# Down weights of the experts issued from ScalarE's DMA queue, gate and up weights from SyncE's

## The reference

```python
def hier_moe(h, ...):
    # top-1 group of 4, then top-2 of the 8 experts in it: gates (tokens x 32)
    for e in range(32):
        hid = silu(t @ w_gate[e]) * (t @ w_up[e])     # (512, 1024) @ (1024, 512), twice
        y = y + gates[:, e:e + 1] * (hid @ w_down[e]) # (512, 512) @ (512, 1024)
```

## Time and profile before

| what | value |
|---|---|
| three runs | 1262.97, 1267.99, 1271.01 us |
| profiled execution: own time / span | 1260.54 / 1258.7 us |
| mean granted TensorE clock | 0.946 |
| busy share of PE, DVE, ACT, POOL | 86, 34, 26, 23 % |
| read from HBM, written | 265.45 MB, 14.63 MB |
| transfers issued by SP (q1) | 114168 packets, 254.15 MB |
| transfers issued by ACT (q10) | 5248 packets, 10.49 MB |
| transfers issued by POOL (q0) | 4992 packets, 13.37 MB |

### The profile page before, as it was taken

How to read it: one execution, slowest core, us unless ns; L and a number is a source line. 1 busy time by engine, 2 the same in 40 slices (tenths; PEclk the granted TensorE clock), 3 DMA queues, 4 the chain that set the end, 5 groups by cost and what they waited for, 6 DMA issues and landing times.

```text
span 1258.7 us, 13952 instructions
## 1 busy us (share of the span) xinstructions
PE 1082.9 (86%) x5506; PEld 695.9 (55%) x5506; DVE 431.1 (34%) x783; ACT 327.9 (26%) x571; POOL 293.1 (23%) x195
## 2 busy tenths in 40 slices
PE   3999999999999999889999559987878878778881
PEld 2778899777789888768867413322222222222220
DVE  3222594488870232359982710000000000000003
ACT  5343642333332544452231301111011011011000
POOL 4332243432224433374440210000000000000002
PEclk8999999999999999999989769999898989889996
DMA  6222223312224522243354749999999999999965
GB/s 155 67 68 67 68 68 101 84 51 67 67 56 146 166 68 68 67 151 100 100 234 200 218 164 402 409 412 419 414 411 418 419 413 415 404 405 412 424 269 207
DMA packets 124455, 278.63 MB, mean 221 GB/s; under 512 B 11561, under 2 KB 97593, under 8 KB 108025
## 3 DMA queue, kind: packets, MB, share of 16 engines
q1 hardware_dynamic: 114168, 254.15, 54.8%
q0 software_dynamic: 4992, 13.37, 3.1%
q10 hardware_dynamic: 5248, 10.49, 2.2%
HBM read 265.45 MB, written 14.63 MB: 223 GB/s over the span
## 4 chain that ended last, share of the span: by engine, by line
PE 60%; DMA 27%; DVE 5%; issue 2%; ACT 2%; POOL 2%; SPq 1%; POOLq 0%; ACTq 0%; DVEq 0%
DMA arena<-w_exp_up_in 25%; PE bank L451 15%; PE bank L472 13%; PE bank L783 10%; PE bank L689 6%; PE bank L746 3%; PE bank L796 2%; DVE work L1239 2%; PE bank L519 1%; PE bank L630 1%; PE bank L587 1%; PE bank L647 1%; POOL piece_r L1614 1%; PE bank L576 1%; DVE piece_r L1348 1%
## 5 line engine op out<-in xcount | busy, mean ns | idle before, releaser
L783 PE MATMUL bank<-arena,work 128*64 128x512 f32 x1024 | 253.7, 653 | 62.5 <-DMA arena<-w_exp_up_in 61.6
L1588 POOL TENSOR_TENSOR piece_r<-arena,piece_r 128x1024 fp32r<-128x1024 f32 x84 | 202.0, 2413 | 384.6 <-ACT piece_r L864 384.6
L451 PE MATMUL bank<-piece_r 128*128 128x512 f32 x960 | 238.0, 399 | 0.0
L783 PEld LDWEIGHTS bank<-arena,work 128*64 128x64 f32 x1024 | 78.8, 150 | 235.3 <-issue 229.2
L451 PEld LDWEIGHTS bank<-piece_r 128*128 128x128 f32 x960 | 175.5, 188 | 41.8 <-issue 7.4
L1502 DVE TENSOR_TENSOR work<-work,bank 128x256 f32<-128x256 f32 x32 | 13.5, 422 | 455.6 <-ACT work L1089 455.6
L472 PEld LDWEIGHTS bank<-piece_r 128*128 128x128 f32 x1344 | 162.1, 192 | 7.4 <-issue 7.4
L472 PE MATMUL bank<-piece_r 128*128 128x256 f32 x1344 | 165.4, 284 | 0.0
L796 PE MATMUL bank<-arena,work 128*64 128x512 f32 x512 | 116.9, 598 | 15.2 <-ACT work L1091 14.7
L864 ACT ACTIVATE piece_r<-arena 128x1024 fp32r<-128x1024 f32 x84 | 88.6, 1057 | 145.1 <-DMA arena<-w_in_in 81.9
L1646 POOL DMA_INDIRECT arena<-h_rows,idx_all x32 | 29.6, 926 | 405.5 <-PE bank L775 402.7
(11 more groups left out here) (230 smaller groups left out, 940.3 us busy)
## 6 DMA issues: line engine op xcount, KB each, us to landing
arena<-w_exp_gate_in SPq DMA_DIRECT2D x32, 2048.0 KB, 31.5
arena<-w_exp_up_in SPq DMA_DIRECT2D x32, 2048.0 KB, 37.9
arena<-w_exp_down_in SPq DMA_DIRECT2D x32, 2048.0 KB, 38.9
arena<-w_in_in SPq DMA_DIRECT2D x68, 512.0 KB, 3.9
y_rows<-work ACTq DMA_DIRECT2D x64, 96.0 KB, 7.6
arena<-w_branch_gla_in SPq DMA_DIRECT2D x8, 512.0 KB, 3.9
arena<-w_branch_dsa_in SPq DMA_DIRECT2D x8, 512.0 KB, 5.1
arena<-w_out_in SPq DMA_DIRECT2D x2, 2048.0 KB, 8.6
```

Source lines behind the costliest of these rows:

```text
L451: last = mm(bank[n % 2][:, :], w[:, k, :], h[:, k, :], start=(i == 0 and k == 0), stop=(i == 2 and k == K - 1))
L783: last = mm(bank[0][hf * WIDE:(hf + 1) * WIDE, :], hTe[sl][:, k, :], wgu[sl][2][:, :, k, hf * HALF:(hf + 1) * HALF], start=(k == 0), stop= ...
L1588: Q.tensor_tensor(quarter(w_lo, q), quarter(w_raw, q), quarter(w_hi, q).bitcast(F32), ALU.subtract).then_inc(s["wlo_ready"], 1)
```

## The change

SP's loop keeps the gate and up loads and loses the wait for `y_ready` and the down load. ACT issues the down load of expert e+3 right behind its wait for `y_ready` of expert e, which is ahead of its wait for `y_stored`, its copy of the product and its two stores. The down loads of experts 0, 1 and 2 stay with SP. ACT's loop is shortened by one round, and its last five experts stand in straight code, the last three of them without a load.

```diff
@@ SP
                 for sl in range(3):
                     sp.wait_ge(s["gu_ready"], e + (sl - 2))
                     load_up(e + sl, sl)
-                    sp.wait_ge(s["y_ready"], e + (sl - 2))
-                    load_down(e + sl, sl)
             for sl in range(2):
                 sp.wait_ge(s["gu_ready"], E3 + sl - 2)
                 load_up(E3 + sl, sl)
-                sp.wait_ge(s["y_ready"], E3 + sl - 2)
-                load_down(E3 + sl, sl)
@@ ACT
-            def run_expert(e, sl, rounds):
+            def run_expert(e, sl, rounds, load_next=True):
...
                 act.wait_ge(s["y_ready"], e + 1)
+                if load_next:
+                    act.dma_start(wdn[sl].rearrange("p (h c) d -> p h c d", h=2),
+                                  wdd[bass.ds(e + 3, 1)].rearrange("e p h c d -> p (e h) c d"))\
+                        .then_inc(wdn_loaded[sl], 16)
                 act.wait_ge(y_stored[sl], rounds * 32 + 32)
                 A(y_sb[sl], bank[1][:, :], ACT.Copy).then_inc(s["act_s"], 1)
                 act.wait_ge(s["act_s"], e + (T + 1))
                 store_y(e * SLOTS, sl, y_stored[sl])
 
-            with act.Fori(0, E3 // 3) as r:
+            with act.Fori(0, E3 // 3 - 1) as r:
                 for sl in range(3):
                     run_expert(r * 3 + sl, sl, r)
-            for sl in range(2):
-                run_expert(E3 + sl, sl, E3 // 3)
+            for e in range(E3 - 3, NE):
+                run_expert(e, e % 3, e // 3, load_next=(e + 3 < NE))
```

## The result

| | us |
|---|---|
| before, median of 18 runs | 1263.35 (1259.52 to 1271.01) |
| changed, median of 18 runs | 1270.24 (1267.82 to 1279.35) |
| ratio, 95% interval | 1.0065 (1.0048 to 1.0081) |
| profiled execution, own time / span | 1268.80 / 1267.0 |

The change costs 0.65% by the ratio, 8.2 us of 1263.35 (6.1 to 10.2); the two medians as they stand are 6.9 us apart. The forecast was +8.9 us, and a span of 1267.6 us. The forecast median of 1277 is 6.8 us too high: 4.6 of them come from the first three runs of before, whose median of 1268 it was added to, and the rest from the 8.9.

A forecast was written before the change was run, and what follows sets the result against it. It took the expert stage to be bound by weight bytes at 411 GB/s, plus PE's work left afterwards. All terms were 0 except the late down loads at the end: 1268.0 + 8.9 = 1277 us median, range 1264 to 1287.

The forecast's parts named there:

- Losing SP's wait gains nothing: SP's loop: dropping the 121.7 us of y_ready waits at L396 issues no gate or up load earlier; worth 0.
- ACT's 29 issues are covered: ACT's expert loop: 29 issues at 0.38 us, 11 us, fit in 6.3 us free per expert; cost 0.
- The bytes end at the same time: Expert stage: the same 201 MB move at 411 GB/s, so weight transfers still end at 1222.5 us.
- The queues take turns, packet for packet, and ACT's queue falls behind: DMA queues: 256 turns of SP's queue pass only 256 of ACT's 352 packets, so down loads fall 96 behind each expert.
- PE pays at the end: Last experts: late down weights leave PE computing alone after the transfers; +8.9 us, bounds -5.8 and +16.2.
- The worked case: PE gets expert 28's down weights at t; transfers end t + 25.5, last down product starts t + 40.2, 1237.2 us.
- first rival: Last experts: down loads get more than needed, up loads come last; +3 to +8 us, 1274 us; chance 0.18.
- The middle costs nothing: Middle of the expert stage: while any queue has work, the bytes lose no time, so PE's waits there cost nothing.
- Down loads ahead: ACT's queue gets more than its need, so up loads come last; +3 to +8 us, 1274 us; chance 0.18.
- Nothing changes: Expert stage: arrival order stays close to need, sum 0, 1268 us; chance 0.12.
- Stores stuck: ACT's queue: stores wait behind down loads and stall ACT, from landings of about 52 us; 1286 us; chance 0.12.
- Faster bytes: Weight transfers: two queues reach 422 GB/s, saving 12.2 us; 1256 us at best, some 1265; chance 0.08.

The follow-up runs named there:

- act_issue_only: Kernel before, plus straight code for ACT's last five experts and a 4 KB dummy DMA issue where the down load would go; ratio 1.0005 to before.
- tail_on_sp: Changed kernel, but SP again issues the down loads of experts 28 to 31, in order of need; ratio 1.0031 to before, stage 479.8 us.
- stores_on_sp: Changed kernel, but SP issues each expert's two stores behind the gate and up loads; ratio 1.0035 to before, stage 484.5 us.
- small_after: Changed kernel, with each gate and up load split in two, 512 pieces of 8 KB per expert; ratio 1.0086 to before, stage 488.5 us.
- store_first: Changed kernel, but ACT issues the down load behind the product's copy and two stores; ratio 1.0057 to before, stage 486.6 us.
- small_before: Kernel before, with each gate and up load split in two, all loads on SP's queue; ratio 0.9999 to before, stage 478.3 us.
- tail_on_act: Kernel before, with only the down loads of experts 28 to 31 moved to ACT; ratio 1.0032 to before, stage 483.9 us.

## Why the prediction was right

Point by point, by its own steps:

- *Losing SP's wait gains nothing.* Right: SP's waits at L392 grew from 263.0 to 421.9 us, more than it had waited at L392 and L396 together (384.7), and a gate load still goes out right behind the product that it waits for (product over at 1191.85, issue at 1191.88).
- *ACT's 29 issues are covered.* Right, by act_issue_only. In the changed kernel they took 0.40 to 0.44 us each, and no long one of 2.7 us occurred.
- *The bytes end at the same time.* Right, 411 GB/s both times, end at 1221.5 against 1222.5 us.
- *The queues take turns, packet for packet, and ACT's queue falls behind.* Right, shown by changing the numbers twice and by the equal counts, 473 against 469. The Trainium skill's page "DMA: Bandwidth & Descriptors", section on queues, rings and completion order, states round robin at packet granularity, with some 9 to 17 descriptors to a packet. Both flips agree with the turns; how many rows make one turn no run here shows, only that it is equally many on both queues. By the rule in its section "Issuing engines are not separate DMA queues", that issuing from several engines only saves sequencer time, the change would have been worth 0: the engines and their throughput are shared as it says, but the time differs by 8 us, since the order of landing is not kept.
- *PE pays at the end.* Right in kind, and in size by the luck of two errors that nearly cancel. The worked case: down product of 28 at t, that of 31 at t + 40.2, transfers over at t + 25.5. Measured with t = 1195.34: t + 41.1 and t + 26.2. Expert 29's down product came 14.56 us behind that of 28, so the late load cost 2.1 us above the pace of 12.44, not 2.9. (The profile's 2.60 us of idle time hold the 0.47 that pass before a down product anyway.) What was left out is the clock: after that wait the product took 5.35 us instead of 3.65 (+1.7), at a granted clock of 0.50 from 1212 to 1214 us, a term the prediction used only in its first rival. 2.1 + 1.7 + 3 x 12.44 are the 41.1. The last down product starts 15.0 us behind the end of the transfers instead of 14.7, and as that end came 1.0 us earlier than before, the loss is 8.1 instead of 8.9.
- *The middle costs nothing.* Right, by tail_on_sp's 73 us of waits for 0.3 us of stage.
- *The rivals.* Down loads ahead: refuted here, but it is what stores_on_sp and small_after do, for +5.0 and +9.0 us of stage against before, where the prediction gave it +3 to +8. Nothing changes: refuted, the interval of the ratio leaves out 1. Stores stuck: they did get stuck (38.4 us, up to 55.2) and did not cost, by store_first. The longest passed the 52 us at which the prediction let them decide, and still ACT lost no more than 0.12 us to one, as PE itself was then waiting for down weights: the down product behind which ACT stood at 1087 had waited 4.52 us for its load. Faster bytes: no, 411 GB/s as before.

## What to carry to other kernels

Here the DMA engines were full (share 1.00), and splitting one ordered stream over two queues changed only who landed first. The queue with more packets for each piece of work landed last, and size did not matter for that: in small_after it was SP's queue with 512 packets of 8 KB, beside 352 of 8 and 2 KB. So count the packets of each queue, not bytes. 73 us of waits in the middle of this stage cost 0.3 us; the price was what the compute engine still had to do when the last byte landed. So keep the tail in the order of need, and try to cut the last load so that compute can start on a part of it. Read who waits for whom together with the landing times: 61.6 us of waits became 78.5 here, and neither figure says anything of the loss.

## What was not expected

**Loads in 512-byte packets are held up beside a write in 4 KB packets.** In the profile of small_before one `w_in` load took 17.7 us, where the median is 3.9, while POOL's zeros went out. The landings of its weight quarters, the queues from 405 to 411 us (q0 is POOL's; packets, MB, share), and the stretches (us, PE, PEld, DVE, ACT, POOL, clock, DMA share, GB/s):

```profile
DMA to landing us min/median/max: 3.6/3.9/17.7
```

```profile
q0 software_dynamic: 461, 1.89, 76.8%
q1 hardware_dynamic: 465, 0.23, 12.9%
```

```profile
413.00:418.00 5.00, 3.93 (x18) 2.88 (x16) 0.59 (x3) 0.60 (x1) 0.00 (x0) 1.00 1.04 341
418.00:423.00 5.00, 2.56 (x7) 1.69 (x8) 1.50 (x7) 4.97 (x10) 3.07 (x2) 0.71 0.59 149
423.00:428.00 5.00, 5.00 (x15) 3.89 (x14) 0.00 (x0) 2.32 (x5) 5.00 (x3) 0.61 0.00 0
```

Again the packets are equally many, and SP's queue moves an eighth of the bytes. PE stands idle for 3.5 us, and its granted clock falls to 0.61 of full speed for 5 us. The profiles of tail_on_sp and store_first show the same (17.9 us both, PE busy 6.61 and 6.48 of 10 us from 413 on), and these three are the ones whose expert stage starts at 756.5 us or later. In the other nine the longest load took 8.2 to 14.0 us, PE was busy for all of those 10 us but 0.04, and the stage starts before 752.

Which course a run takes goes with a race of half a microsecond at 398 us. In the three late ones POOL's zeros are issued 0.05 to 0.44 us ahead of SP's `w_in` load of that moment; in tail_on_act, with the 14.0 us, 0.01 behind it; in the other six with one large write, 0.31 to 0.58 behind. That these courses make a part of the scatter between runs fits the eight smaller writes (range 4.4 instead of 9.6 us); it rests on one profile of each kernel.

**A wait of PE often costs twice.** After waits of 2.60 and 3.69 us 16 matmuls took 5.35 and 5.18 instead of 3.65 us. In the kernel before, all 13 waits of 2.43 us and more ahead of the gate and up products were followed by 32 matmuls that took 8.41 to 10.03 us, and all seven shorter ones by 7.09. In the earlier trace rows the clock granted during such a product is 0.50, its 1.2 GHz level. It is no fixed rule of the length: in stores_on_sp a wait of 2.03 us was followed by 8.79 us and one of 2.21 by 7.09, and in small_after one of 3.81 by 7.09.
